# A hybrid layer and two transformer blocks on one NeuronCore: two key products written for each weight once, the copy to the other partitions by DMA, and one norm entered earlier

## The reference, cut to what matters

```python
(aq, ak, av, iq, ik, iw, bq, ...) = split_cols(h @ w_in)      # ik: 64 columns, iw: 8 columns
o_a = dsa_attention(aq, ak, av, iq, ik, iw, rel_bias)
...
kv = rms_norm(x, kv_norm) @ w_kv                             # before feed-forward layer 2
k_flat, v_flat = jnp.split(kv, 2, axis=-1)                   # 256 columns each: 4 heads of 64
x = x + 0.5 * swiglu(rms_norm(x, ffn_norm[i, 0]), ...)       # feed-forward layer 2
q = rms_norm(x, mix_norm[i]) @ b_w_q                         # 16 heads of 64
z = jnp.einsum('bqkgd,bskd->bkgqs', q, k)
```

## Time and profile before

| | |
|---|---|
| median of 3 runs | 2121.45 us (2120.76, 2122.81, 2121.45) |
| profiled execution, first to last instruction | 2120.9 us |
| profiled execution, its own time | not shown apart from the span |
| PE busy | 1965.8 us, 93% |
| DVE, ACT, POOL busy | 1144.7, 901.8, 106.5 us |
| mean granted PE clock | 0.978 |

### The profile page before, as it was taken

How to read it: one execution, slowest core, us unless ns; L and a number is a source line. 1 busy time by engine, 2 the same in 40 slices (tenths; PEclk the granted TensorE clock), 3 DMA queues, 4 the chain that set the end, 5 groups by cost and what they waited for, 6 DMA issues and landing times.

```text
span 2120.9 us, 28563 instructions
## 1 busy us (share of the span) xinstructions
PE 1965.8 (93%) x11768; PEld 1547.3 (73%) x11768; DVE 1144.7 (54%) x1553; ACT 901.8 (43%) x1277; POOL 106.5 (5%) x94
## 2 busy tenths in 40 slices
PE   9999999999999766667679999999999999999998
PEld 8999888889997211111138888888888888988887
DVE  6656684576764110111017666665666766766666
ACT  4544455454443100000015556645545654576454
POOL 0233111000210000000000000000000000000000
PEclk9999999999999989998899999999999999999999
DMA  9533543566987999999996755544655555524652
GB/s 374 167 120 120 179 150 133 191 217 233 307 325 315 390 424 423 423 424 423 422 406 220 243 185 179 179 159 159 209 188 179 179 179 191 167 80 151 216 180 80
DMA packets 242153, 503.04 MB, mean 237 GB/s; under 512 B 9698, under 2 KB 158531, under 8 KB 217571
## 3 DMA queue, kind: packets, MB, share of 16 engines
q1 hardware_dynamic: 241344, 500.53, 64.5%
q10 hardware_dynamic: 530, 0.47, 0.1%
q0 software_dynamic: 144, 0.17, 0.1%
HBM read 500.07 MB, written 1.06 MB: 236 GB/s over the span
## 4 chain that ended last, share of the span: by engine, by line
PE 74%; DMA 16%; DVE 5%; ACT 3%; issue 1%; SPq 1%; POOL 0%; DVEq 0%; ACTq 0%
PE bank L578 14%; PE bank L580 14%; PE bank L579 14%; PE bank L639 13%; DMA m<-in_expert_w_up 8%; DMA m<-in_expert_w_down 7%; PE bank L641 7%; PE bank L998 2%; PE bank L1009 2%; PE bank L746 1%; DVE m L2155 1%; PE bank L885 1%; DMA m<-in_ffn_w_in 1%; DVE m L2278 1%; DMA m<-in_ada_w 0%
## 5 line engine op out<-in xcount | busy, mean ns | idle before, releaser
L2155 DVE TENSOR_TENSOR m<-m,m 128x1024 fp32r<-128x1024 f32 x508 | 619.0, 1232 | 287.9 <-ACT m L1479 286.8
L578 PE MATMUL bank<-m,m 128*128 128x256 f32 (+1 forms) x1992 | 671.3, 337 | 9.7 <-DVE m L2155 4.8
L580 PE MATMUL bank<-m,m 128*128 128x256 f32 (+1 forms) x1992 | 656.9, 330 | 0.0
L579 PE MATMUL bank<-m,m 128*128 128x256 f32 (+1 forms) x1992 | 656.3, 329 | 0.0
L1479 ACT ACTIVATE m<-m 128x1024 fp32r<-128x1024 f32 x508 | 526.8, 1053 | 240.7 <-PE bank L580 214.0
L639 PE MATMUL bank<-m,m 128*128 128x512 f32 x1248 | 439.8, 394 | 0.0
L578 PEld LDWEIGHTS bank<-m,m 128*128 128x128 f32 x1992 | 377.3, 189 | 56.2 <-DVE m L2155 11.1
L580 PEld LDWEIGHTS bank<-m,m 128*128 128x128 f32 x1992 | 377.4, 189 | 36.8
L579 PEld LDWEIGHTS bank<-m,m 128*128 128x128 f32 x1992 | 377.8, 190 | 35.6 <-issue 2.4
L641 PE MATMUL bank<-m,m 128*128 128x256 f32 x1248 | 352.7, 283 | 0.0
L639 PEld LDWEIGHTS bank<-m,m 128*128 128x128 f32 x1248 | 234.4, 188 | 54.0
(11 more groups left out here) (358 smaller groups left out, 1462.0 us busy)
## 6 DMA issues: line engine op xcount, KB each, us to landing
m<-in_ffn_w_in SPq DMA_DIRECT2D x88, 1024.0 KB, 5.0
m<-in_expert_w_gate SPq DMA_DIRECT2D x64, 1024.0 KB, 24.6
m<-in_expert_w_up SPq DMA_DIRECT2D x64, 1024.0 KB, 23.6
m<-in_w_in SPq DMA_DIRECT2D x63, 1024.0 KB, 4.9
m<-in_expert_w_down SPq DMA_DIRECT2D x60, 1024.0 KB, 25.4
m<-in_ffn_w_out SPq DMA_DIRECT2D x44, 1024.0 KB, 4.8
m<-in_ada_w SPq DMA_DIRECT2D x24, 1024.0 KB, 5.5
m<-in_a_w_in SPq DMA_DIRECT2D x16, 1024.0 KB, 5.2
```

What stands on the lines that cost most here:

```text
L578: e.matmul(o, s[0], m[0], start=first, stop=False, skip_group_check=skip)
L579: e.matmul(o, s[0], m[1], start=False, stop=False, skip_group_check=skip)
L580: return e.matmul(o, s[1], m[0], start=False, stop=last, skip_group_check=skip)
L2155: inc(e.tensor_tensor(rv(fit(q.L, q.view.shape)), q.view, fit(q.H, q.view.shape), ALU.subtract), "l", skey(q, "L"))
```

## The change

- `ik` and `iw` are one piece of 72 columns and one product: 24 matmuls give the key on partitions 0 to 63 and the index weights, transposed, on 64 to 71. ACT takes both out with two instructions and issues a DMA that copies the key to partitions 64 to 127. PE turns the weights back with two small transposes at the start of `attention`, and ACT scales them there.
- `kk` is two pieces of two heads each, 48 matmuls into bank 4. DVE takes them out with two instructions of 64 partitions x 512; at step 0 of `stick` ACT issues two DMAs that copy each head to the other 64 partitions. `stick_logits` waits for them ("kkd").
- `enter(nm[1], 0)` moves into `last_outs` of `ffn(2, nm[1])`, on all engines; the bank turn is set to 0 ahead of that layer and `q0` uses bank 2.
- There are three fewer pieces, so that the slots behind them shift by one or three, and `p.after` goes by slot.

```diff
-        G["ik"] = [Piece(plan, ld, w3[:, :, 0:64].unsqueeze(2).to_broadcast([128, 8, 2, 64]), 1024)]
-        G["iw"] = [Piece(plan, ld, w3[:, :, 64:72], 64)]
+        G["ik"] = [Piece(plan, ld, w3, 576)]
...
-        ld = load(lambda r: r.rearrange("p (k n) -> p k n", n=256), wkv[:, 0:256].rearrange("(k p) n -> p k n", p=128))
-        G["kk"] = [Piece(plan, ld, ld.raw.rearrange("p (k n) -> p k n", n=256)[:, :, 64 * j:64 * j + 64]
-                         .unsqueeze(2).to_broadcast([128, 8, 2, 64]), 1024, g=j) for j in range(4)]
+        plan_gemm2("kk", wkv, 8, [0])
...
-        for i, p in enumerate(plan[first_ffn:first_ffn + NH]):
-            p.after = ("exu", 7, 3 if i < 2 else 4)
+        for p in plan[first_ffn:first_ffn + NH]:
+            p.after = ("exu", 7, 3 if p.slot < 2 else 4)
...
+        iwT = mem(52656, 256)[64:72]
...
+        kk_of = [[kk[64 * i:64 * i + 64].rearrange("p (b h n) -> p h b n", b=2, h=2)[:, h] for h in range(2)] for i in range(2)]
... (PE)
             def attention():
+                w.wait_ge("iwT")
+                b = take("s", "iw")
+                for t in range(2):
+                    ins = e.transpose(b[:, 8 * t:8 * t + 8], iwT[:, 128 * t:128 * t + 128], K(C_ID)[64:72, 64:72])
+                full(ins, "iw")
                 yield
...
                         w.wait_ge("ik")
+                        w.wait_ge("ik2")
...
                 w.wait_ge("qq", j)
-                w.wait_ge("kk2", 3)
+                w.wait_ge("kk2")
+                w.wait_ge("kkd")
...
-                    ins = three(b[:, 0:256], parts(p, 128 * k, 128), (hT[0][:, k, :], hT[1][:, k, :]), k == 0, k == 7)
+                    ins = three(b[0:72, 0:256], parts(p, 72 * k, 72), (hT[0][:, k, :], hT[1][:, k, :]), k == 0, k == 7)
...
-            for p in walk("iw"):
-                ...
-                    for k in range(8):
-                        ins = three(b[:, 0:8], (hT[0][:, k, rows], hT[1][:, k, rows]), parts(p, 8 * k, 8), k == 0, k == 7)
...
-            ffn(2)
+            turn["m"] = 0
+            ffn(2, nm[1])
             for p in walk("kk"):
                 w.wait_ge(*skey(p, "L"))
-                if p.g in (1, 2):
-                    enter(nm[1], p.g - 1)
-                b = take("m", "kk2", p.g)
+                if p.b:
+                    enter(nm[1], 1)
+                else:
+                    b = take(4, "kk2")
                 for k in range(8):
                     w.wait_ge("kv", k // 2)
-                    ins = three(b[:, 0:256], parts(p, 128 * k, 128), (kvT[0][:, k, :], kvT[1][:, k, :]), k == 0, k == 7)
-                used(ins, p, ("kk2", p.g))
+                    ins = three(b[:, 256 * p.b:256 * p.b + 256], parts(p, 128 * k, 128), (kvT[0][:, k, :], kvT[1][:, k, :]),
+                                k == 0, k == 7)
+                used(ins, p, *([("kk2",)] if p.end else []))
...
-                gemm2(f"q{i}", nm[1].T, m1_ready, at=(3, 7, 3, 3)[i],
+                gemm2(f"q{i}", nm[1].T, m1_ready, at=(2, 7, 3, 3)[i],
... (ACT)
             def attention():
+                b = got("iw")
+                taken(e.activation(iw, b[:, 0:16], ACT.Copy, scale=float(512) ** -0.5), "iw", also=[("iws",)])
                 yield
...
                 for step in range(16):
+                    if step == 0:
+                        w.wait_ge("kk2")
+                        for i in range(2):
+                            then_inc(e.dma_start(kk_of[1 - i][i], kk_of[i][i]), "kk_over", ("kkd",), by=16)
...
-                taken(e.activation(ik, b[:, 0:256], ACT.Copy), "ik", also=[("ik",)])
-            for p in walk("iw"):
-                ...
+                inc(e.activation(ik[0:64], b[0:64, 0:256], ACT.Copy), "ik", ("ik",))
+                taken(e.activation(iwT, b[64:72, 0:256], ACT.Copy), "ik", also=[("iwT",)])
+                w.wait_ge("ik")
+                then_inc(e.dma_start(ik[64:128], ik[0:64]), "ik_over", ("ik2",), by=16)
... (DVE)
-            ffn(2, keep=True)
+            ffn(2, nm[1], keep=True)
...
-                if p.g in (1, 2):
-                    entered(nm[1], p.g - 1)
-                ev_kk(p)
+                if p.b:
+                    entered(nm[1], 1)
+            b = got("kk2")
+            for i in range(2):
+                r = slice(64 * i, 64 * i + 64)
+                ins = e.tensor_tensor(kk_of[i][i], v256(b[r, :]), nf[2].row[r].unsqueeze(1).to_broadcast([64, 2, 256]), ALU.mult)
+            taken(ins, "kk2", also=[("kk2",)])
```

More of the change, by code:

```diff
@@ L1374, in tensor @@
                 for k in range(8):
-                    ins = three(b[:, 0:256], parts(p, 128 * k, 128), (hT[0][:, k, :], hT[1][:, k, :]), k == 0, k == 7)
+                    ins = three(b[0:72, 0:256], parts(p, 72 * k, 72), (hT[0][:, k, :], hT[1][:, k, :]), k == 0, k == 7)
                 used(ins, p, ("ik",))
-            for p in walk("iw"):
[L1378 to L1381, removed]
-                    for k in range(8):
-                        ins = three(b[:, 0:8], (hT[0][:, k, rows], hT[1][:, k, rows]), parts(p, 8 * k, 8), k == 0, k == 7)
-                used(ins, p, ("iw", 0), ("iw", 1))
             gemm2("aq", hT, h_ready)
@@ L2306, in attention @@
                 w.wait_ge("aM")
-                w.wait_ge("iw", 1)
+                w.wait_ge("iws")
                 for i in range(2):
@@ L2968, in vector @@
             run("ik")
-            run("iw")
             run("aq")
@@ L3305, in sync @@
             then_inc(e.dma_start(aO[0:32, :], a["buckets"]), "rel_in", ("rel_bias",), by=16)
-            run("bi", "iq", "ik", "iw", "aq")
+            run("bi", "iq", "ik", "aq")
             w.wait_ge("aU")
```

## The result

| kernel | median us | runs, lowest to highest | ratio to before, 95% interval |
|---|---|---|---|
| before | 2121.11 | 4, 2120.49 to 2122.81 | |
| after | 2106.57 | 4, 2106.06 to 2108.21 | 0.9929, 0.9917 to 0.9941 |

The change takes 14.5 us off; 12.3 us and 2109.2 us were forecast. The time lies near the low end of the range. The profiled execution took 2107.03 us with a span of 2105.2, 15.7 us less than the span of before.

A forecast was written before the change was run, and what follows sets the result against it. PE was taken to bound the kernel (93% busy), the experts' weights being on DMA. Index part 7.5 plus key part 4.8 gives 12.3 us off the 2120.9 span, 2108.6, plus 0.55: 2109.2 us, range 2106.2 to 2115.2.

The forecast's parts named there:

- The step that failed: First attention's side-job levels: interval over the index weights falls from 12.96 to 8.04 us, 4.92 less, later spacing unchanged.
- the index part: Index keys and weights of the first attention: 7.9 us less 0.4 for transposes, net 7.5 us, bounds 5.0 and 8.5.
- the first interval: Level-to-level distance over the index weights: 4.92 us less, plus 0.12 at the level after it.
- Index weights: Removing the 48 narrow matmuls and their slot, half clock behind them included, saves 7.9 us before the transposes' cost.
- One piece less behind the last level: What the levels' chain holds back of the index weights' gain comes behind the last level: 2.88 us.
- Clock falls anyway: Rival at the index keys: a piece still runs at 1.2 GHz, 2.4 to 2.5 us kept, 2111.7 us; chance 0.08.
- Key pieces: Second attention's keys: two pieces go, 5.76 us, less waits and a split, net 4.8 us, bounds 0.9 and 5.8.
- T: Time when PE's transposes of the norm's second half, ahead of the second attention's key pieces, are done; 1835.79 before.
- Late copy: Rival at the second attention's logits: key copies land 7.3 us after issue, 3.8 us more waiting, 2113.0 us; chance 0.13.
- slower through it: Rival: copies land 13.3 us after issue, PE stands 10.4 us, then half clock; 13.4 more, 2122.6 us; chance 0.04.
- Experts swallow the first part: Rival at the DMA-bound experts: the index part's 7.5 us turn into waiting there, 2116.7 us; chance 0.05.

The follow-up runs named there:

- before_late_tick: The kernel before with one empty step ahead of the levels' program on all four engines, nothing else: 2117.58 us, ratio 0.9983 to before.
- late_tick: The changed kernel with one empty step ahead of the levels' program on all four engines, nothing else: 2108.63 us, ratio 0.9944 to before.
- small_run: The changed kernel with the 48 matmuls of 8 columns put back as one run behind the index keys' piece: 2113.84 us, ratio 0.997 to before.
- small_mixed: The changed kernel with the 48 matmuls of 8 columns put back, six behind every three wide ones: 2114.35 us, ratio 0.9969 to before.
- b_only: The kernel before with only the second attention's key change (two pieces, DMA copy, norm entered sooner): 2115.77 us, ratio 0.9978 to before.
- pool_copy: The changed kernel with the two copies of the second attention's keys issued by GpSimd instead of ACT: 2105.69 us, ratio 0.9932 to before.
- best: The changed kernel with first-half retention output copied out one step sooner, GpSimd issuing key copies, the first behind half the eviction: 2102.77 us.

## Why the prediction was right or wrong, point by point

- **The step that failed** is the sentence "the levels hang on a chain through ACT and DVE, which does not get shorter: the interval falls from 12.96 to 8.04". That chain begins with ACT's place in the round of pairs, and removing one piece shifted it. The interval fell to 7.58 and then stayed at 7.5. Of the 2.75 us by which the index part was forecast too small (10.25 against 7.5), 2.46 is the stretch between the levels, net of 1.3 us lost between its two halves, and 0.34 the first interval (5.38 against 4.92 + 0.12). before_late_tick puts the price at 3.1 us by its median; late_tick puts it at 2.5 by its median and 1.35 by its trace. The evidence was in the trace of before: ahead of the level at 120.46 PE waits 0.28 us for DVE, and that DVE product starts behind ACT's exponentials, which start behind the copy out of a pair. I followed the wait one step back and took it for fixed.
- **Index weights, other terms.** The 128x8 rows are gone and the clock is 1.00, as forecast; small_run puts run and clock together at 7.96 us against 7.9. The reading that the clock was 1.00 while the 48 matmuls ran, 0.12 us each, was not exact: 43 of them stand 0.11 us apart, and the last five, from 135.12 on, 0.21 us apart at half clock. The sum is untouched, since it goes from start to start. The two transposes (L779, at 224.76, busy for 0.29 us) cost some 0.4 us with the gaps around them (0.4 forecast). One piece less behind the last level gave 2.41 net of them, forecast 2.88 - 0.4.
- **Clock falls anyway**: did not happen at the index keys. The Trainium skill ("TensorE: Matmul & The Clock Gate", Part 1) ties the lower clock to idleness; by it the run of narrow matmuls should not have brought it, and small_run and small_mixed show that it did with PE never idle in the profile.
- **Key pieces.** 5.76 less the waits was forecast at 4.8; measured 4.55 between the marks, 4.9 by b_only's median. The wait at the logits is 0.95, forecast 0.6, and in this part it is the term that was mis-sized: ACT's issues took 0.65 us each where I took SP's 0.51, and DVE had the keys' eviction done at T+7.27 (forecast T+7.2), the last split begun at T+9.90 and `q0` out at T+11.7 (forecast T+11.2, though its terms add up to 11.1), with T = 1821.78.
- **Late copy, and slower through it**: the copies landed 2.4 and 2.5 us after their issue, as forecast (2.2). The fit of the Trainium skill ("DMA: Bandwidth & Descriptors", "Anatomy of one DMA") that the prediction uses for ACT's copy is stated there for DMAs issued from GpSimd. The copies were hidden in after, but only just: the second landed at about 1832.2, and PE stood idle from 1832.61 for `q0`; in pool_copy, with the other wait gone, they are what PE waits for.
- **Experts swallow the first part**: did not happen. The 11.8 us by which the attention's logits stand sooner are 11.1 at layer 0's rounding. The slots cost nothing: ACT waits there for weights by 13.38 us, as with the earlier trace rows.
- **The sum against one span.** The span of before held 1.5 us of half clock at its start that other executions don't have. The forecast's base, that span and 0.55 us, is the median of the runs shown, so the stretch is not in its error; but 15.7 us between two spans would have been read as the change's.

## What to carry to other kernels

When a piece of work is taken out of a loop in which a side job takes turns with it, work out again on which turn the side job now falls on each engine: what stood behind a copy or an eviction may come free of it, or the reverse, and here that was worth about a fifth of what the change gained. Follow a small recurring wait back through every engine before calling its period fixed; an empty turn, put in on purpose, tests it in one run. Where two inputs of an instruction are late by about the same amount, removing the lateness of one shows nothing; count both before judging either.

## What the runs showed of the hardware

- Matmuls of 8 moving columns with 128 x 128 stationary tiles follow each other by 0.11 us at the full clock (126.02, 126.13, 126.24 in small_run), next to 0.12 for 256 columns, and by 0.21 us at half clock (135.34, 135.55 in before). The weight loads stand at the same distance (timeline of weight loads in small_run):

```profile
126.77 0.19 PEld L579 LDWEIGHTS bank<-m,m 128*128 128x128 f32 x1
126.88 0.19 PEld L577 LDWEIGHTS bank<-m,m 128*128 128x128 f32 x1
126.99 0.19 PEld L578 LDWEIGHTS bank<-m,m 128*128 128x128 f32 x1
```

- The granted clock fell to 0.50 with no idle time of PE in the profile, behind or among such matmuls, for 6.8 us in before and small_run and 10.0 in small_mixed and before_late_tick. What exactly the chip reacts to was not varied further and stays open, and so does what sets the length of the stretch.
- A copy of 128 KB between partitions landed 2.3 to 2.5 us after its issue from ACT or, in best, from GpSimd; of two issued back to back by GpSimd the later took 3.3 us (pool_copy).
